# Gathering expert rows as quarter rows of a permuted copy, and turning them on VectorE instead of TensorE

## The chip, the cores and the metric
One NeuronCore of a Trainium2 chip runs the whole program. The metric is the device time of one execution in microseconds. TensorE multiplies matrices, VectorE and ScalarE do element-wise work, GpSimd issues the indirect transfers (gathers and adds by row number), SyncE issues the plain ones.

## The reference
One decoder layer over 1024 tokens of width 1024, in float32. A mixer (gated convolution, stick-breaking attention, gated linear attention, one output projection) is followed by `x1 = layer_norm(ALPHA * x + mix)`. Then a mixture of experts and a second layer norm:

```
scores = sigmoid(x1 @ router_w);  the best of 4 groups, the best 2 of its 4 experts
gate   = scores of the two, divided by their sum
for e in range(16):                       # every expert, D_EXPERT = 512
    h = silu(x1 @ w1[e]) * (x1 @ w3[e])
    y += gate[:, e] * (h @ w2[e])
out = layer_norm(ALPHA * x1 + y)
```

## The kernel before
The change touches the part behind the mixer. It has four stages.

Output projection and first layer norm: 8 tiles of 128 tokens. VectorE writes x1 (two buffers), SyncE stores each tile twice (`store_x1`): to `x1_scratch`, from which rows are gathered, and to `sum_scratch`, to which the experts' results are added.

Routing: VectorE computes for each token its two experts, the position of the token in each expert's list and the gates. An expert has 160 slots per pass (`TW`): 128 of them are the rows, 32 the spare slots (`TR`). For experts 0 to 2 (`DIRECT`) the lists are formed on the core itself: `slot_hits` compares positions with slot numbers (one-hot, `oneh`), `slot_tokens` on TensorE multiplies the one-hot by the token numbers, `slot_rows` on VectorE turns the sums into row numbers firstA and firstB. For experts 3 to 15 GpSimd scatters token numbers and gates to a table in DRAM (`scatter`, 16 indirect DMAs of 128 entries) and loads it back expert by expert (`load_table`).

Expert blocks: one block per expert, in order, each with the same list on each engine. The spare slots are computed differently from the rows: 32 slots leave three quarters of TensorE's output partitions unused, so four column groups of the weights run side by side (`spare_gu`, `spare_y`; quarter g of the output width stands on partitions 32g to 32g+31). Their x comes by quarter rows: partition 32g+s has columns 256g to 256g+255 of slot s's token (xgB, [128 x 256]). The rows come whole (xgA, [128 x 1024]). Products of the rows are made of three terms, hi by hi, hi by lo and lo by hi; the hi part of each 512 KB weight piece (12 pieces per expert) is made by ScalarE (`piece_hi`, eh), the lo part by VectorE (`piece_lo`, el), and for x there are xh and xl.

TensorE's list in a block b (`pe_block`): `spare_gu`; `rows_gu` of w1, then of w3; transpose of hB; transposes of the next expert's xgA (8, `x_transposes` rounds 0 and 1); transposes of hA (4); transposes of the next xgB (2, round 2); `spare_y`; the down products of the rows. ScalarE copies each transposed round out (`x_hi`, xh and xB) and VectorE forms xl (`x_lo`). VectorE's list: el of pieces 4 and 5, hB, el of 6 to 11, hA, hTl, xl of the next expert, el of its pieces 0 to 3, yA.

GpSimd's list in a step (`step`): load the table of expert b (one DMA of 128 entries, four of 32), copy the gates of expert b-2, compute the quarter ids, gather expert b's rows (xgA, xgB) as soon as the transposes of expert b-1 have read the buffer, then add the results of expert b-2 to `sum_scratch` (`add_rows`: yB, yA). Each instruction waits in this order. Gathers run two blocks ahead of their use; from expert 2 on one buffer serves them all.

Weights: SyncE loads piece p of the next expert when el and the raw products of piece p are done (`load_expert`).

The last block (`pe_last`, `dve_last`, `act_last`) runs beside the second layer norm, which starts when the adds of expert 14 have landed.

## Time and profile before

| | us |
|---|---|
| median of 3 runs | 970.53 (970.23 to 974.96) |
| span of the profiled execution | 966.3 |
| TensorE busy in the span | 915.8 |
| VectorE busy | 610.2 |
| ScalarE busy | 483.7 |
| GpSimd busy | 205.4 |
| mean granted TensorE clock, share of full | 0.985 |

The span runs from the first to the last instruction; the page gives no other time of that execution. The times of the runs are those of the whole device execution. Busy times of the engines overlap. The projections and the mixer take the first 425 us, the output projection until 525, routing until 550, the expert blocks until about 940.

### The profile page before, as it was taken

How to read it: one execution, taken by the hardware profiler on the slowest of the kernel's cores; microseconds unless marked ns; L12 is line 12 of the kernel's file. 1: busy time of each engine (PE TensorE's matmuls, PEld its weight loads, DVE VectorE, ACT ScalarE, POOL GpSimd, SP SyncE). 2: the span in 40 equal slices, each digit the busy share in tenths (PEclk: the TensorE clock that was granted, in tenths of full speed). 3: DMA queues.
4: the chain of work that ended last, by engine and by line, in shares of the span. 5: the costliest groups of instructions: out<-in, count | busy, mean ns of one | idle time of the engine just before them, and what ended most of it. 6: DMA issues, size and time to landing. Idle time of an engine off the chain costs nothing.

```text
span 966.3 us, 17168 instructions
## 1 busy us (share of the span) xinstructions
PE 915.8 (95%) x6403; PEld 720.1 (75%) x6403; DVE 610.2 (63%) x812; ACT 483.7 (50%) x779; POOL 205.4 (21%) x242
## 2 busy tenths in 40 slices
PE   8999999999999999979999899999999999999980
PEld 7778998996777777767887577777777777777760
DVE  4212833665665655677655897777777777777786
ACT  3312532225564654562222436666666666666674
POOL 3000000000000000040000186434334444444144
PEclk9999999999999999999999899999999999999995
DMA  9301120001100031049532289999999999999974
GB/s 262 70 22 44 45 61 27 1 2 44 44 22 23 23 77 44 1 137 361 214 113 100 91 203 314 371 338 320 317 316 319 324 318 318 321 318 315 321 257 169
DMA packets 102668, 168.81 MB, mean 175 GB/s; under 512 B 25532, under 2 KB 49212, under 8 KB 102608
## 3 DMA queue, kind: packets, MB, share of 16 engines
q1 hardware_dynamic: 88720, 143.74, 44.0%
q0 software_dynamic: 10848, 23.09, 9.8%
q10 hardware_dynamic: 3040, 1.19, 0.6%
q8 instruction: 37, 0.61, 0.3%
q14 instruction: 23, 0.19, 0.1%
HBM read 143.76 MB, written 24.54 MB: 174 GB/s over the span
## 4 chain that ended last, share of the span: by engine, by line
PE 85%; DVE 7%; ACT 3%; DMA 3%; issue 1%; POOL 0%; SPq 0%; ACTq 0%; POOLq 0%; DVEq 0%
PE bank L866 14%; PE bank L868 13%; PE bank L867 13%; PE pz L866 7%; PE pz L867 7%; PE pz L868 7%; PE pz L1216 6%; PE pz L1242 3%; PE pz L982 3%; PE bank L1060 3%; PE bank L1076 2%; PE bank L1204 1%; DVE el L1955 1%; DMA x_row<-in_x_dram 1%; PE bank L1015 1%
## 5 line engine op out<-in xcount | busy, mean ns | idle before, releaser
L1955 DVE TENSOR_TENSOR el<-er,eh 128x1024 fp32r<-128x1024 f32 x192 | 225.5, 1222 | 49.7 <-ACT eh L1556 48.8
L1556 ACT ACTIVATE eh<-er 128x1024 fp32r<-128x1024 f32 x192 | 190.2, 1052 | 8.6 <-PE pz L868 8.6
L1887 DVE TENSOR_TENSOR_SCAN Qs<-Qs,own 128x128 f32<-128x128 f32 (+7 forms) x48 | 65.0, 1355 | 69.7 <-ACT Qs L1443 69.7
L866 PE MATMUL bank<-xT_hi,w_hi 128*128 128x512 f32 (+1 forms) x264 | 105.6, 400 | 1.9 <-DVE xT_lo L1772 1.9
L868 PE MATMUL bank<-xT_hi,w_lo 128*128 128x512 f32 (+1 forms) x264 | 101.7, 385 | 0.0
L866 PE MATMUL pz<-eh,xh 128*128 128x512 f32 x256 | 101.6, 397 | 0.0
L867 PE MATMUL bank<-xT_lo,w_hi 128*128 128x512 f32 (+1 forms) x264 | 101.1, 383 | 0.0
L867 PE MATMUL pz<-el,xh 128*128 128x512 f32 x256 | 99.8, 390 | 0.0
L868 PE MATMUL pz<-eh,xl 128*128 128x512 f32 x256 | 99.7, 389 | 0.0
L629 POOL MEMSET rw<- 128x128 f32 x1 | 0.2, 205 | 413.4 <-DVE mix L1880 413.4
L866 PE MATMUL bank<-w_hi,xT_hi 128*128 128x384 f32 x192 | 65.0, 338 | 1.3 <-ACT kteN L1458 1.3
L868 PE MATMUL bank<-w_hi,xT_lo 128*128 128x384 f32 x192 | 64.2, 335 | 0.0
L867 PE MATMUL bank<-w_lo,xT_hi 128*128 128x384 f32 x192 | 64.2, 334 | 0.0
L1216 PE MATMUL pz<-er,xB 128*32 128x256 f32 x1024 | 60.5, 388 | 0.5 <-ACT xB L1603 0.5
L866 PEld LDWEIGHTS pz<-eh,xh 128*128 128x128 f32 x256 | 48.0, 188 | 16.2 <-issue 6.2
L866 PEld LDWEIGHTS bank<-xT_hi,w_hi 128*128 128x128 f32 x264 | 49.8, 189 | 11.8 <-DVE xT_lo L1772 2.1
L868 PEld LDWEIGHTS bank<-xT_hi,w_lo 128*128 128x128 f32 x264 | 49.6, 188 | 10.5
L867 PEld LDWEIGHTS bank<-xT_lo,w_hi 128*128 128x128 f32 x264 | 49.8, 189 | 8.6
L868 PEld LDWEIGHTS pz<-eh,xl 128*128 128x128 f32 x256 | 48.1, 188 | 10.2
L867 PEld LDWEIGHTS pz<-el,xh 128*128 128x128 f32 x256 | 48.1, 188 | 9.3
L866 PE MATMUL bank<-eh,hTh 128*128 128x512 f32 x128 | 51.8, 405 | 0.0
L1216 PEld LDWEIGHTS pz<-er,xB 128*32 128x32 f32 x1024 | 32.0, 111 | 26.3 <-issue 6.9
(336 smaller groups left out, 1808.5 us busy)
## 6 DMA issues: line engine op xcount, KB each, us to landing
er<-in_w_dram SPq DMA_DIRECT2D x192, 512.0 KB, 8.9
w_raw<-in_w_in_dram SPq DMA_DIRECT2D x21, 512.0 KB, 3.9
x_row<-in_x_dram SPq DMA_DIRECT2D x8, 512.0 KB, 9.0
xres<-in_x_dram SPq DMA_DIRECT2D x8, 512.0 KB, 5.4
x_scratch<-x SPq DMA_DIRECT2D x8, 512.0 KB, 2.6
sum_scratch<-x SPq DMA_DIRECT2D x8, 512.0 KB, 3.9
cx<-sum_scratch SPq DMA_DIRECT2D x8, 512.0 KB, 8.6
out_dram<-cx SPq DMA_DIRECT2D x5, 512.0 KB, 3.0
```

The lines of the kernel that those rows point to most:

```text
L866: pe.matmul(dst, lh, rh, start=(k == k_first), stop=False)
L867: pe.matmul(dst, lh, rl, start=False, stop=False)
L868: last = pe.matmul(dst, ll, rh, start=False, stop=(k == k_last))
L982: last = pe.matmul(pz[h][:, c:e], q[r, 0, own], q[r, 1, c:e], start=True, stop=True)
L1015: pe.matmul(pa_[:, h * GLA_DV:(h + 1) * GLA_DV], sT[:, h % 2, h // 2, :], gv[:, c, h * GLA_DV:(h + 1) * GLA_DV], start=(h == 0), stop=Fals ...
L1060: last = pe.matmul(po[64 * h:64 * h + 64, 0:P], sv[keys, j, (2 * p + h) * SB_D:(2 * p + h + 1) * SB_D], aT[keys, h, j, :], start=(j == 0), ...
L1076: last = pe.transpose(tr_bank[g % 2][:, (j % 4) * P:(j % 4 + 1) * P], Bs[:, n % 2, h, j * P:(j + 1) * P], ident[:, :])
L1216: last = pe.matmul(guB[g * TR:(g + 1) * TR, :].rearrange("p (m f) -> p m f", m=2), xB[:, k, :], both, start=(k == 0), stop=(k == NK - 1), ...
L1242: last = pe.matmul(yB_bank[g * TR:(g + 1) * TR, :], hTB[:, f, :], er[:, p, g * DQ:(g + 1) * DQ], start=(f == 0), stop=(f == NF - 1), skip_ ...
L1556: act.activation(eh[:, p, :], er[:, p, :], ACT.Copy).then_inc(S["eh_ok"], 1)
L1887: dve.tensor_tensor_scan(Qs[:, h, 0:W][:, ::-1], Qs[:, h, 0:W][:, ::-1], own1[:, T - W:][:, ::-1], 0.0, ALU.mult, ALU.max).then_inc(S["sca ...
L1955: dve.tensor_tensor(el[:, p, :], er[:, p, :], eh[:, p, :].bitcast(F32), ALU.subtract).then_inc(S["el_ok"], 1)
```

## The change
x1 is stored to `x1_scratch` with its columns permuted: ScalarE copies each tile (`x1_blocked`) so that quarter g of a stored row holds, for each of the 8 blocks of 128 columns, its columns 32g to 32g+31. All rows are then gathered as quarter rows: partition 32g+s of part c has quarter g of slot 32c+s. There are NB = 5 parts of [128 x 256] per expert, four for the rows and one (the last) for the spare slots, each an indirect DMA of its own. Each 32x32 block then has to be turned in place only, and VectorE's transpose does that: `spare_turn` writes xB, `rows_turn` writes xT, in one instruction each. The TensorE transposes of xgA and xgB go away, and with them ScalarE's copies from PSUM; `x_hi` is one copy of 1024 columns, `x_lo` one subtraction.

In routing, hits, token sums and row numbers are formed in two parts, the spare slots first, and token numbers are summed for each of the five parts on four partition groups (160 small matmuls per expert instead of 40). The tables have all five parts' entries on each partition. Some empty matmuls (`spin`) are added. TensorE's list in a block becomes: `spare_gu`, `rows_gu` of w1, transpose of hB, `rows_gu` of w3, half of `spare_y`, transposes of hA, the other half, hi products of the first two down pieces, then their lo products, then the rest.

```diff
-        xgAs = [rt("xgA0", 6 * K, [P, D]), rt("xgA1", 42 * K, [P, D])]
+        xg = [rt("xg0", 6 * K, [P, NB, DQ]), rt("xg1", 42 * K, [P, NB, DQ])]
+        xT = rt("xT", 16 * K, [P, NK, P])
...
+            def store_blocks(i):
+                sp.wait_ge(S["x1p_ok"], i + 1)
+                sp.dma_start(x1_dram[i * P:(i + 1) * P, :], x1p[:, i % 2, :]).then_inc(S["x1p_st"], 16)
...
             def first_gather(b):
+                pool.wait_ge(S["first_ok"], 2 * b + 1)
+                pool.indirect_dma_start(xg[b % 2][:, NB - 1, :], None, x1_quarters, bass.IndirectOffsetOnAxis(firstQ[:, b, NB - 1:NB], 0))\
+                    .then_inc(S["xgB_in"], 16)
                 pool.wait_ge(S["first_ok"], 2 * b + 2)
+                for c in range(NB - 1):
+                    pool.indirect_dma_start(xg[b % 2][:, c, :], None, x1_quarters, bass.IndirectOffsetOnAxis(firstQ[:, b, c:c + 1], 0))\
+                        .then_inc(S["xg_in"], 16)
 
             first_gather(0)
-            pool.wait_ge(S["xg_in"], 16)
+            pool.wait_ge(S["xgB_in"], 16)
+            pool.wait_ge(S["xg_in"], 16 * (NB - 1))
             first_gather(1)
             scatter(0)
             scatter(1)
...
             def load_table(r, b):
                 for g in range(NQ):
-                    pool.dma_start(tab[r][g * TR:(g + 1) * TR, 2:4], idl_dram[bass.ds(b * TW + P, TR), :]).then_inc(S["idx_in"], 16)
+                    pool.dma_start(tab[r][g * TR:(g + 1) * TR, 2:].rearrange("s (c o) -> s c o", c=NB),
+                                   idl_dram[bass.ds(b * TW, TW), :].rearrange("(c s) o -> s c o", c=NB)).then_inc(S["idx_in"], 16)
...
             def gather(r, b, buf=0, ready=None):
-                pool.indirect_dma_start(xgAs[buf][:, :], None, x1_dram, bass.IndirectOffsetOnAxis(tab[r][:, 0:1], 0)).then_inc(S["xg_in"], 16)
-                pool.indirect_dma_start(xgBs[buf][:, :], None, x1_quarters, bass.IndirectOffsetOnAxis(tabQ[r][:, 0:1], 0)).then_inc(S["xg_in"], 16)
+                pool.indirect_dma_start(xg[buf][:, NB - 1, :], None, x1_quarters, bass.IndirectOffsetOnAxis(tabQ[r][:, NB - 1:NB], 0))\
+                    .then_inc(S["xgB_in"], 16)
+                for c in range(NB - 1):
+                    pool.indirect_dma_start(xg[buf][:, c, :], None, x1_quarters, bass.IndirectOffsetOnAxis(tabQ[r][:, c:c + 1], 0))\
+                        .then_inc(S["xg_in"], 16)
...
+            def spare_turn(b, buf):
+                dve.wait_ge(S["xgB_in"], 16 * b + 16)
+                if not first_block(b):
+                    dve.wait_ge(S["raw_done"], NPIECE * (b - 1) + 2 * NF)
+                dve.transpose(xB[:, :, :].rearrange("p k s -> p (k s)"), xg[buf][:, NB - 1, :]).then_inc(S["xBt_ok"], 1)
+
+            def rows_turn(b, buf):
+                dve.wait_ge(S["xg_in"], 16 * (NB - 1) * b + 16 * (NB - 1))
+                if not first_block(b):
+                    dve.wait_ge(S["piece_done"], (NPIECE - 1) * (b - 1) + 2 * NF)
+                dve.transpose(xT[:, :, :].rearrange("p k (c s) -> p c k s", c=NB - 1),
+                              xg[buf][:, 0:NB - 1, :].rearrange("p c (k r) -> p c k r", k=NK)).then_inc(S["xTt_ok"], 1)
...
             def dve_block(b, nxt, buf=0, nbuf=0):
                 dve.tensor_tensor(hB[:, :], silB[:, :], guB[:, P:2 * P], ALU.mult).then_inc(S["hB_ok"], 1)
+                if nxt and not first_block(b):
+                    spare_turn(b + 1, nbuf)
                 piece_lo(b, 6)
                 piece_lo(b, 7)
...
                 dve.tensor_tensor(hA[:, :], silA[:, :], uA, ALU.mult).then_inc(S["hA_ok"], 1)
                 if first_block(b):
                     piece_lo(b, NPIECE - 2)
+                    spare_turn(b + 1, nbuf)
+                if nxt:
+                    rows_turn(b + 1, nbuf)
                 dve.wait_ge(S["hTh_ok"], b + 1)
```

## Rows read from the trace of the kernel before

**Rows 1.** The page: busy us, share of the span, instructions.

```profile
PE 915.8 (95%) x6403; PEld 720.1 (75%) x6403; DVE 610.2 (63%) x812; ACT 483.7 (50%) x779; POOL 205.4 (21%) x242
```

**Rows 2.** Chain of waits, spare products of experts 1 and 14: start, us, what.

```profile
580.81 3.59 PE pz L1216 x64
...
891.38 3.59 PE pz L1216 x64
```

**Rows 3.** Timeline of TensorE, end of a block: start us, us, group.

```profile
786.57 1.03 PE L1204 MATMUL bank<-ident,xgA 128*128 128x128 f32 x8
787.44 0.61 PE L1301 MATMUL pz<-ident,hA 128*128 128x128 f32 x4
787.89 0.38 PE L1204 MATMUL pz<-ident,xgB 128*128 128x128 f32 x2
788.20 1.93 PE L1242 MATMUL pz<-er,hTB 128*32 128x256 f32 x32
...
795.75 3.66 PE L1216 MATMUL pz<-er,xB 128*32 128x256 f32 x64
```

**Rows 4.** Stretches: length, busy (x) of PE, PEld, DVE, ACT, POOL; clock, DMA, GB/s.

```profile
549.00:556.00 7.00, 6.04 (x82) 3.28 (x80) 5.58 (x23) 0.60 (x2) 2.72 (x3) 0.54 0.48 128
...
604.70:628.60 23.90, 23.90 (x188) 17.97 (x191) 17.45 (x19) 15.53 (x21) 10.45 (x12) 1.00 1.05 370
...
867.50:891.40 23.90, 23.90 (x187) 17.97 (x191) 17.52 (x19) 15.61 (x21) 10.33 (x11) 1.00 0.95 315
```

**Rows 5.** Timeline of VectorE in the same blocks; in brackets the idle time before.

```profile
786.65 0.69 DVE L2219 TENSOR_TENSOR hA<-silA,pz 128x512 f32<-128x512 f32 x1 [1.51 <-PE pz L868]
...
799.80 0.28 DVE L2205 TENSOR_TENSOR hB<-silB,pz 128x128 f32<-128x128 f32 x1
800.74 4.63 DVE L1955 TENSOR_TENSOR el<-er,eh 128x1024 fp32r<-128x1024 f32 x4 [0.65 <-ACT eh L1556]
```

**Rows 6.** Timeline of GpSimd, gathers of experts 2 and 3 and between.

```profile
582.56 2.04 POOL L689 DMA_INDIRECT xgB<-x_scratch,firstB  x1 [0.30 <-issue]
...
590.12 1.20 POOL L723 DMA_DIRECT2D tab<-slot_tokens  x1
590.72 2.64 POOL L725 DMA_DIRECT2D tab<-slot_tokens  x4
600.09 0.68 POOL L731 TENSOR_SCALAR tabQ<-tab,quad 128x1 uint32<-128x1 uint32 x1 [6.73 <-DMA tab<-slot_tokens]
601.63 1.18 POOL L739 DMA_INDIRECT xgA<-x_scratch,tab  x1 [0.86 <-POOL tabQ L731]
...
605.31 1.63 POOL L707 DMA_INDIRECT sum_scratch<-yB,addB  x1 [0.30 <-issue]
...
608.53 1.21 POOL L723 DMA_DIRECT2D tab<-slot_tokens  x1
...
617.77 0.30 POOL L731 TENSOR_SCALAR tabQ<-tab,quad 128x1 uint32<-128x1 uint32 x1 [6.00 <-DMA tab<-slot_tokens]
```

**Rows 7.** Scatters (ns min/median/max, first and last start), and timelines beside el.

```profile
L678 POOL DMA_INDIRECT slot_tokens<-tokg,rows_u x16: 968/1097/2034, 556.2 to 581.3; - x16
...
576.68 2.03 POOL L678 DMA_INDIRECT slot_tokens<-tokg,rows_u  x1 [0.30 <-issue]
579.02 1.97 POOL L678 DMA_INDIRECT slot_tokens<-tokg,rows_u  x1 [0.31 <-issue]
...
576.65 4.62 DVE L1955 TENSOR_TENSOR el<-er,eh 128x1024 fp32r<-128x1024 f32 x4
```

**Rows 8.** Timelines of GpSimd, VectorE and TensorE at the first block.

```profile
552.91 1.03 POOL L689 DMA_INDIRECT xgB<-x_scratch,firstB  x1 [3.89 <-DMA xgA<-x_scratch,firstA]
...
556.41 1.29 DVE L1961 TENSOR_TENSOR xl<-bank,xh 128x512 fp32r<-128x512 f32 x2 [1.31 <-ACT xh L1603]
...
557.98 0.50 PE L866 MATMUL pz<-eh,xh 128*128 128x512 f32 x1
```

**Rows 9.** DMA issues: KB, median us from issue to landing.

```profile
xgB<-sum_scratch,tabQ POOLq DMA_INDIRECT x1, 6.6
```

More of the change, by code:

```diff
@@ L258, in build @@
         oneb = small("oneb", [P, P], BF16)
-        tab = [small(f"tab{r}", [P, 4], U32) for r in range(4)]
-        tabQ = [small(f"tabQ{r}", [P, 1], U32) for r in range(4)]
+        tab = [small(f"tab{r}", [P, 2 + 2 * NB], U32) for r in range(4)]
+        tabQ = [small(f"tabQ{r}", [P, NB], U32) for r in range(4)]
         slotGs = [small(f"slotG{r}", [P, 2]) for r in range(2)]
@@ L277, in build @@
         addB = small("addB", [P, DIRECT], U32)
[L278 to L281 removed]
+        assert place[0] <= R + 53 * K, place[0] - R - 53 * K
         selm = at("selm", C0 + 5760, [P, P])
@@ L318, in build @@
         oneh = rt("oneh", 24 * K, [P, 2, NT, TW], BF16)
+        place[0] = M + 29 * K
+        sids = small("sids", [P, DIRECT, NB])
+        firstQ = small("firstQ", [P, DIRECT, NB], U32)
+        sidA = small("sidA", [P, DIRECT])
+        assert place[0] <= M + 30 * K
         er = at("er", R, [P, NPIECE, D])
@@ L1189, in _, with spare_gu @@
             slot_gates(0)
+            spin(4, po[:, 0:GLA_W])
             slot_tokens(1)
             slot_gates(1)
-            def x_transposes(b, rounds, buf=0):
-                xgA, xgB = xgAs[buf], xgBs[buf]
-                if first_block(b) and rounds == (2,):
-                    pe.wait_ge(S["xgB_in"], 16)
-                else:
-                    pe.wait_ge(S["xg_in"], 32 * b + 16)
-                for r in rounds:
-                    for d in range(4 if r < 2 else 2):
-                        rows = xgA[:, (4 * r + d) * P:(4 * r + d + 1) * P] if r < 2 else xgB[:, d * P:(d + 1) * P]
-                        last = pe.transpose(xb[r][:, d * P:(d + 1) * P], rows, ident[:, :])
-                    last.then_inc(S["xtr_ps"], 1)
-            def spare_gu(b, part=None):
-                for q in range(NF) if part is None else range(2 * part, 2 * part + 2):
+            spin(4, po[:, 0:GLA_W])
+            def spare_gu(b):
+                pe.wait_ge(S["xBt_ok"], b + 1)
+                for q in range(NF):
                     for p in (q, NF + q):
@@ L1302, in pe_block, with products @@
                 last.then_inc(S["hTA_ps"], 1)
-                if nxt:
-                    x_transposes(b + 1, (2,), nbuf)
-                spare_y(b)
-                pe.wait_ge(S["hTl_ok"], b + 1)
-                if not first_block(b):
+                spare_y(b, range(2, NF))
+                if first_block(b):
+                    pe.wait_ge(S["first_ok"], 6)
+                else:
                     pe.wait_ge(S["yA0_ev"], b)
                     pe.wait_ge(S["yA1_ev"], b)
-                for f in range(NF):
+                pe.wait_ge(S["hTh_ok"], b + 1)
+                def products(f, half, low):
                     p = 2 * NF + f
-                    pe.wait_ge(S["el_ok"], NPIECE * b + p + 1)
-                    for half in range(2):
-                        last = mm3(pe, pp[half][:, :], 0, NF - 1, lambda f: (hTh[:, f, :], hTl[:, f, :]),
-                                   lambda f: (k_of(eh, p, half), k_of(el, p, half)), [f])
+                    if low:
+                        last = pe.matmul(pp[half][:, :], hTl[:, f, :], k_of(eh, p, half), start=False, stop=(f == NF - 1))
                         if f == NF - 1:
@@ L1320, in pe_block @@
                             last.then_inc(S["piece_done"], 1)
+                    else:
+                        pe.matmul(pp[half][:, :], hTh[:, f, :], k_of(eh, p, half), start=(f == 0), stop=False)
+                        pe.matmul(pp[half][:, :], hTh[:, f, :], k_of(el, p, half), start=False, stop=False)
+                for f in range(2):
+                    pe.wait_ge(S["el_ok"], NPIECE * b + 2 * NF + f + 1)
+                    for half in range(2):
+                        products(f, half, False)
+                pe.wait_ge(S["hTl_ok"], b + 1)
+                for f in range(2):
+                    for half in range(2):
+                        products(f, half, True)
+                for f in range(2, NF):
+                    pe.wait_ge(S["el_ok"], NPIECE * b + 2 * NF + f + 1)
+                    for half in range(2):
+                        products(f, half, False)
+                        products(f, half, True)
             def pe_pass(j):
-                if isinstance(j, int):
-                    pe.wait_ge(S["first_ok"], 4)
-                    x_transposes(0, (2,))
-                else:
+                if not isinstance(j, int):
                     pe.wait_ge(S["hA_ok"], NE * j)
-                    x_transposes(NE * j, ROUNDS_FIRST)
                 experts_of(pe, j, pe_block, pe_last)
```

255 lines of the change are left out of this document (128 added, 127 removed).

## The prediction
> **What bounds the kernel now.** I read the page's busy shares first: TensorE is busy for 95% of the span [rows 1]. Then the loop over the 16 experts, because the change touches that and the short stage ahead of it. The chain of waits runs through TensorE: its 64 spare-slot products start at 580.81 us for expert 1 and at 891.38 for expert 14 [rows 2], so a block takes (891.38 - 580.81) / 13 = 23.89 us. The timeline of TensorE across the end of a block shows no gap [rows 3]. The other engines and the transfers have room: VectorE is busy 17.5 us of a block, and the load is 315 GB/s where the same loop reached 370 in an earlier block [rows 4]. So the loop is as long as TensorE's instruction list, as long as what feeds it comes in time. What feeds it is a long line of steps on GpSimd (table load, gather, adds of an earlier expert), hidden today.
>
> **Part 1, what TensorE loses.** Eight transposes of xgA run from 786.57 to 787.44, two of xgB from 787.89 to 788.20 [rows 3]: 0.87 + 0.31 = 1.18 us per block. A block that only TensorE limits takes 23.89 - 1.18 = 22.71 us. The removed work also covered waits, so I go through the new order. After the last gate/up product VectorE needs about 1.0 us for hA (the transposes of hA start at 787.44, hA at 786.65 [rows 3, 5]); two quarters of spare_y (half of its 1.87 to 1.93 us, 0.93 [rows 3]) now stand there, a loss of at most 0.1. The other half stands behind the transposes of hA, while ScalarE copies hTh. Eight hi products (8 x 0.23 = 1.8 us) stand before hTl is wanted. VectorE puts the new turn of the rows between hA and hTl: the turn may take about 2.5 us before TensorE notices. x1's permuted copy costs ScalarE one more 1024-column copy per tile in a stage in which it is idle most of the time: nothing, and its store replaces one that was there.
>
> **Part 2, what VectorE gains.** No 32x32 turn is in the trace. The nearest rows are 1024-column operations in SBUF, el at (4.63 / 4) 1.16 us [rows 5]; upper end: twice that, 2.3 us, if the type takes two passes; lower end half of it, 0.6 us, if two columns go at once. I take 1.2 for the rows and, with a quarter of the columns, 0.4 for the spare slots. xl becomes one operation instead of two, the same time. VectorE then works 17.5 + 1.6 = 19.1 of 22.7 us: it fits. The Trainium skill ("Vector Engine (DVE) Microarchitecture Reference", 3.8 The reshape front-end) says that the transpose sustains one element per cycle per lane; that agrees with my middle value, and no run here shows it yet. ScalarE's three copies per block become one over 1024 columns: a small gain, hidden, since ScalarE is busy for 15.6 of 23.9 us [rows 4].
>
> What can hurt is the place of spare_turn in VectorE's queue. It stands behind hB, before el of pieces 6 to 11, and waits for the spare gather of the next expert. hB starts at 799.80, 4.05 us into a block (block start 795.75 [rows 3, 5]). Six el at 1.16 us stand behind it, 7.0 us, and hA is wanted at 14.8 us into the new block (3.6 spare products, 0.1 hB transpose, 11.0 gate/up, 0.1). So spare_turn has to be through by 7.8 us; from there every us is lost by TensorE.
>
> **Part 3, GpSimd, which I hold to be the point that decides.** One step of it, in order: gather (2 issues before, 5 now), add of yB, add of yA, table load, wait for the table, quarter ids. In the one step that waited for nobody else, gathers start at 601.63, the adds at 605.31, the table load at 608.53, the ids at 617.77 [rows 6]: 3.68 for two gathers, 3.22 for the adds (I take 3.3, for the copy of the gates that later steps have beside them), 9.24 for the table (9.97 in the step before it, 590.12 to 600.09; I take the middle, 9.6), and 1.54 from the ids to the next gather (600.09 to 601.63) [rows 6]. Without gathers: 3.3 + 9.6 + 1.5 = 14.4 us. The tables now carry 5 entries per row instead of 1 in four small DMAs; the issue of 128 entries takes 1.20 us and the four of 32 entries take 2.64 together [rows 6], so the 160 entries that each now has cost between nothing and 0.5 us apiece. I take 0.15, nearer to the row in which four times the entries hardly show: 0.6 for the four. Sum 15.0.
>
> What is a gather issue worth? Sixteen scatters of the same form start within 25.1 us, 1.67 apart on the mean, durations 0.97 to 2.03 [rows 7]. The long ones stand where VectorE runs el back to back: 576.68 and 579.02 start inside the run of four el from 576.65 and end 2.3 us apart; where VectorE reads PSUM or is idle the spacing is 1.3 [rows 7]. The Trainium skill ("SBUF — State Buffer", Who interferes with whom) has the rule that a VectorE instruction with two SBUF inputs contends with a GpSimd instruction that reads SBUF; the trace agrees (2.03 against 0.97 us). By it the four new gathers per block cost up to 2.3 each. Bounds for five gathers: 5 x 1.3 = 6.5 and 1.3 + 4 x 2.3 = 10.5. I take 7.8 us: a gather that is late is issued while VectorE itself stands waiting at spare_turn, with only two el in the way. Step: 15.0 + 7.8 = 22.8 us, against 22.71 of TensorE: level, bounds 21.5 and 25.5.
>
> **Part 4, the start.** Before, hi/lo row products start at 557.98, behind xl at 556.41 [rows 8]. After: the spare hits (256 columns compared first instead of 1280 at once) let the first spare gather go about 1.2 us earlier, but the four row gathers follow at 1.3 to 1.5 each behind the rest of the count and land at about 555.5 (before: xgA had landed at 552.9, when GpSimd went on [rows 8]). Then the turn 1.2, the rest of the routing chain and one el that stand between (3.1) and xl (1.2): row products at 561.0, 3.0 us later. Block 0 also gets 120 more small matmuls (about 1 us) and loses the 1.5 us of transposes: it ends at 584 instead of 580.8. TensorE's clock was at half for most of 549 to 556 (0.54 on the mean [rows 4]); the added spins may spare that, the new wait may bring it back: plus or minus 3, taken as none.
>
> GpSimd starts its 16 scatters late: first_gather(1) waits until the first gathers landed (555.5) and issues five (7.5 us): 563 instead of 556.2, so expert 2's gather starts at 589.8 instead of 582.56 [rows 6], and expert 3's at 589.8 + 19.07 (601.63 - 582.56) + 4.4 + 0.6 = 613.9. A gather under load lands 6.6 us after its issue [rows 9], with the mean delay to its wait about 7. So in block 1 spare_turn(2) waits until 596.8, 12.8 us into the block: 5.4 lost. In block 2, spare_turn(3) waits until 620.9; six el, hA, its transposes, spare_y and the down products (5.7, from 790.1 to 795.75 [rows 3]) follow (0.3 + 7.0 + 0.8 + 0.45 + 0.93 + 5.7 = 15.2, less 0.3 of overlap): block 2 ends at 635.8. Twelve blocks at 22.8 follow: block 14 ends at 909.4. Before it ended at 891.38 + 23.89 = 915.3. That is 5.9 us less. The last block and the layer norm behind it have none of the removed work except what block 14 held: unchanged. The span of the profiled execution is 966.3 us; the median of the runs, 970.53, stands 4.2 above it; I take the difference from the median: 970.5 - 5.9 = 964.6 us.
>
> **Rivals.** (A) TensorE's list alone decides: gathers stay at 1.3 apart and the start catches up. Block 0 ends at 584, fourteen blocks at 22.71 end at 901.9: -13.4, 957 us. For it: the low spacing stands in half of the rows. Against: the five gathers in a row at the start. Chance 0.15.
> (B) Slower: GpSimd's line becomes the bound. The new gathers fall on el, 2.3 apart; five take 9.1, the step is 15.0 + 9.1 = 24.1 us or more; block 14 ends at 635.8 + 12 x 24.1 = 925: +9.7, 980 us. The turning point is a step of (915.3 - 635.8) / 12 = 23.3 us, only 0.5 above my sum. Sign of it: VectorE waits in every block at spare_turn, TensorE has gaps ahead of the transposes of hA. By the skill's port rule without the relief that I assumed, this is the outcome. Chance 0.20.
> (C) The turn of [128 x 1024] costs two passes or more (over 2.5 us): hTl is late in each block and the start loses 1 to 3 more: 970 to 985. Chance 0.07.
> (D) Steps level near 23.2: the removed 1.2 us per block are given back to waits, 967 to 972. Chance 0.18.
> My forecast, 0.40, its own range 960 to 968.
>
> **How the numbers follow.** A comparison of such runs tells about 0.5% (4.85 us) from no change. Below 965.7: all of A, two thirds of the forecast and a little more, 0.15 + 0.30; some of the rest lies where the start is cheaper than I made it: 0.47. Above 975.4: B, most of C: 0.27. Between: 0.26. Range: 955 to 981, which leaves a tenth on either side.
>
> **What would show it.** Blocks at 22.7 to 23.0 us instead of 23.89; five gather issues in 6.5 to 8; the ids of the next table 9 to 11 us behind the table load; a stop of VectorE ahead of the [128 x 256] turn in blocks 1 and 2, about 8 us in block 1, and a short one in the later ones; expert 2's first gather near 590. The turn of 1024 columns at 1.1 to 1.3 us. I am wrong if there is no such stop (then A), or if blocks are over 23.3 us (then B).

## The result: 0.7% slower, and the profile after

| us | before | after |
|---|---|---|
| median, 5 runs each on one chip | 970.23 (967.71 to 974.96) | 977.50 (972.44 to 981.02) |
| span of the profiled execution | 966.3 | 979.3 |
| TensorE busy | 915.8 | 913.9 |
| GpSimd busy | 205.4 | 284.0 |
| mean granted clock | 0.985 | 0.973 |

The ratio is 1.0070 [1.0047, 1.0093]: 0.7% slower, with the whole interval above 1. I had forecast 964.6. The profiled execution of the changed kernel is the slowest of its five runs (981.02), so the two spans stand 13.0 us apart and the medians 7.3. The account of the 13.0 us below is one of these two executions.

The page's busy rows of the changed kernel, against [rows 1]; GpSimd has 50 more instructions, TensorE is busy as long as before:

```profile
PE 913.9 (93%) x6611; PEld 707.4 (72%) x6611; DVE 631.5 (64%) x831; ACT 482.2 (49%) x755; POOL 284.0 (29%) x292
```

One block of TensorE, its timeline from one spare_gu to the next, against [rows 3] (the products of the rows are left out). The ten transposes are gone, and in a block that waits for nothing 23.09 us are left of 23.89:

```profile
756.33 3.66 PE L1226 MATMUL pz<-er,xB 128*32 128x256 f32 x64
...
765.50 0.28 PE L1294 MATMUL pz<-ident,hB 128*128 128x128 f32 x1
...
771.16 1.07 PE L1253 MATMUL pz<-er,hTB 128*32 128x256 f32 x16
772.16 0.66 PE L1300 MATMUL pz<-ident,hA 128*128 128x128 f32 x4
772.75 1.07 PE L1253 MATMUL pz<-er,hTB 128*32 128x256 f32 x16
...
779.42 1.93 PE L1226 MATMUL pz<-er,xB 128*32 128x256 f32 x32
```

But many blocks wait. VectorE's waits over blocks 1 to 14 (what, in all us, times, longest): it stands before the turn of the next expert's spare rows, 8.0 us once and 28.2 us in eleven blocks. TensorE pays for the long stops alone: block 1 takes 28.9 us and four later blocks take 24.4, 23.4, 25.4 and 27.0; all others take 23.1.

```profile
DVE xB L1982 <- DMA xg<-x_scratch,tabQ: 28.2, 11, 5.4
...
DVE xB L1982 <- DMA xg<-x_scratch,firstQ: 8.0, 1, 8.0
```

VectorE's timeline has the stop of block 1 and both turns, 0.45 and 1.24 us, against the el beside them [rows 5]:

```profile
601.06 0.45 DVE L1982 STREAM_TRANSPOSE xB<-xg 128x256 f32<-128x256 f32 x1 [8.04 <-DMA xg<-x_scratch,firstQ]
...
771.88 1.24 DVE L1989 STREAM_TRANSPOSE xT<-xg 128x1024 f32<-128x1024 f32 x1
```

GpSimd's timeline of one step, against [rows 6]. The step's first gather started at 734.84; from there 6.8 us of gathers, 4.3 of adds, 9.9 from the table load to the ids, 2.7 from the ids to the next gather. From the first gather of expert 3 to that of expert 15 it waits for nobody but its own table:

```profile
741.62 2.64 POOL L774 DMA_INDIRECT sum_scratch<-yB,tabQ  x1 [0.30 <-issue]
744.56 1.89 POOL L779 DMA_INDIRECT sum_scratch<-yA,tab  x1 [0.30 <-issue]
745.91 1.18 POOL L737 DMA_DIRECT2D tab<-slot_tokens  x1
...
755.77 1.75 POOL L746 TENSOR_SCALAR tabQ<-tab,quad 128x5 uint32<-128x5 uint32 x1 [6.12 <-DMA tab<-slot_tokens]
758.51 1.09 POOL L756 DMA_INDIRECT xg<-x_scratch,tabQ  x1 [0.99 <-POOL tabQ L746]
```

Expert 3's first gather starts at 613.38 and expert 15's at 902.10: 288.72 / 12 = 24.06 us a step, over the 23.89 of the whole block before. Means over these steps: gathers 7.2 us, adds 4.1, table 9.8, ids to gather 2.9.

Where 13.0 us of span went, by the starts of spare_gu in TensorE's timeline (the last column from the prediction's 584, 22.71 + 5.4, and 909.4):

| stretch | before | after | difference | predicted |
|---|---|---|---|---|
| start of block 1 | 580.8 | 587.4 | +6.6 | +3.2 |
| block 1 | 23.9 | 28.9 | +5.0 | +4.2 |
| blocks 2 to 14 | 310.6 | 308.0 | -2.6 | -13.3 |
| block 15 to the last GpSimd issue | 46.1 | 45.7 | -0.4 | 0 |
| last issue to the end of the span | 5.0 | 9.4 | +4.4 | 0 |

### The profile page after: what moved, and what is told of

Same layout as the page of the kernel before. It is cut to its first block, busy times and chain, and to the rows that moved or that the text cites. A ratio compares the mean times of both kernels' runs of the same rounds, so it can differ in the third digit from the quotient of the medians.

```text
span 979.3 us, 17611 instructions
## 1 busy us (share of the span) xinstructions
PE 913.9 (93%) x6611; PEld 707.4 (72%) x6611; DVE 631.5 (64%) x831; ACT 482.2 (49%) x755; POOL 284.0 (29%) x292
## 4 chain that ended last, share of the span: by engine, by line
PE 56%; POOL 16%; DMA 10%; issue 8%; DVE 6%; ACT 3%; POOLq 0%; SPq 0%; DVEq 0%; ACTq 0%
PE bank L887 11%; PE bank L889 11%; PE bank L888 11%; DMA tab<-slot_tokens 9%; PE pz L1003 3%; PE bank L1081 2%; POOL xg L759 2%; POOL tabQ L746 2%; PE pz L887 2%; PE pz L889 2%; PE pz L888 2%; PE bank L1097 2%; POOL sum_scratch L774 2%; POOL sum_scratch L779 2%; POOL slot_tokens L685 2%
## 5 line engine op out<-in xcount | busy, mean ns | idle before, releaser
L887 PE MATMUL pz<-eh,xh 128*128 128x512 f32 x256 | 104.4, 408 | 4.4 <-DVE el L1975 4.4
L759 POOL DMA_INDIRECT xg<-x_scratch,tabQ x52 | 58.3, 1122 | 15.9 <-issue 15.9
L889 PEld LDWEIGHTS bank<-xT_hi,w_lo 128*128 128x128 f32 x264 | 49.9, 189 | 10.6
L889 PEld LDWEIGHTS pz<-eh,xl 128*128 128x128 f32 x256 | 48.6, 190 | 10.6
```

The costliest lines, as they stand in the source:

```text
L759: pool.indirect_dma_start(xg[buf][:, c, :], None, x1_quarters, bass.IndirectOffsetOnAxis(tabQ[r][:, c:c + 1], 0))\
L887: pe.matmul(dst, lh, rh, start=(k == k_first), stop=False)
L889: last = pe.matmul(dst, ll, rh, start=False, stop=(k == k_last))
```

## The experiments

There were 18 runs. Those of one group shared a chip, each group had another one, and each run is compared with the kernel before on its chip. The changed kernel itself ran in the first comparison and in the second group only. "Changed" is the kernel after the change.

### First group: the step of GpSimd, and the place of the turn

**One row gather.** Three of the four row gathers are left out from expert 3 on, so three quarters of xT hold old rows.

```diff
-                for c in range(NB - 1):
+                for c in range(1):
```


> The changed kernel, but from expert 3 on GpSimd issues one row gather instead of four per expert (three quarters of the rows keep what an earlier expert left there; everything else, tables included, is unchanged). Theory 1 (GpSimd's step bounds the loop): its step falls from 24.06 us by three issues of about 1.35, to 20.0; TensorE's own list, 23.1 us per block, decides again and the stops of VectorE at the turn of the spare rows end after block 2: 12 blocks at 23.1 instead of 24.06, some 8 us less than the changed kernel, 969 to 970 us. Theory 2 (only the start costs, the loop is fine): no change, 977. Theory 3 (the loop is slow because the 1 KB rows crowd the DMA queues): also about 8 us less, since 0.38 MB per block goes away with the issues; the next kernel tells 1 from 3.

Measured: 984.84 against 974.07, ratio 1.0104 [1.0069, 1.0139]. It is slower, not 8 us faster, and yet from block 1 on every block takes 23.1 us and no stop at the spare turn is left, as the step theory says. (The theory of crowded transfers says so too; the table a step ahead, below, keeps all transfers and tells them apart.) The loss is in block 0, which took 47.1 us. TensorE's timeline there, in the middle of 200 small products (slot_tokens and slot_gates of expert 2), shows a few at a time:

```profile
577.56 0.22 PE L1191 MATMUL bank<-idb,oneh 128*32 128x2 bf16 x6 [0.51 <-issue]
578.30 0.21 PE L1191 MATMUL bank<-idb,oneh 128*32 128x2 bf16 x4 [0.52 <-issue]
579.01 0.22 PE L1191 MATMUL bank<-idb,oneh 128*32 128x2 bf16 x5 [0.50 <-issue]
...
588.36 0.23 PE L1204 MATMUL bank<-gsplit,oneh 128*32 128x4 bf16 x4 [1.19 <-issue]
```

**Table a step ahead.** The table of expert b+1 is loaded behind the gathers of b, ahead of the adds.

```diff
+                    load_table(0, 4)
...
+                    for b in range(4, NE):
+                        quarters(b % 4, b)
+                        gather(b % 4, b)
+                        if b + 1 < NE:
+                            load_table((b + 1) % 4, b + 1)
+                        if b > 4:
+                            gates((b + 2) % 4, b - 2)
+                            add_rows((b + 2) % 4, b - 2)
...
-                with pool.Fori(2 if isinstance(j, int) else 1, NE // 4) as i:
```

The edit also writes out GpSimd's steps of experts 8 to 15, which had been a loop. That is not what shortens the step: in the changed kernel the steps written out (first gather of expert 3 to that of expert 8, 613.38 to 734.84) take 24.3 us each and those in the loop (734.84 to 902.10) 23.9.

> The changed kernel with GpSimd's list reordered: the table of the next expert is loaded right behind the gathers and ahead of the two adds, so that its landing (9 to 10 us from the issue) passes beside the adds. Same transfers, same bytes, same number of issues. Theory 1: the step becomes ids 2.9 + gathers 7.1 + table issue 3.6 + adds 4.3 + a rest of the landing of about 2 = 20 us, below TensorE's 23.1; about 8 us less than the changed kernel, 969 to 970. Theory 2 (start only) and theory 3 (queues crowded by small rows): no change, 977.

Measured: 1028.62, ratio 1.0557. Block 0 took 46.5 us; blocks 1 to 3 took 23.1 to 23.3, the later ones 27.2 (the last 24.3). That was my edit: gates(b-2) now stood behind the gather of b, which waits for the rows' turn, and ScalarE's yB waits for those gates. Its waits:

```profile
ACT yB L1653 <- POOL slotG L764: 81.3, 10, 8.1
```

**Spare turn late.** spare_turn moves from behind hB to behind hA.

```diff
-                if nxt and not first_block(b):
-                    spare_turn(b + 1, nbuf)
...
                 if nxt:
+                    spare_turn(b + 1, nbuf)
                     rows_turn(b + 1, nbuf)
```


> The changed kernel with the turn of the spare rows moved in VectorE's list from ahead of the six el to behind hA, next to the turn of the rows. GpSimd's step stays at 24 us. Theory 1: the stop of 8 us in block 1 no longer reaches TensorE (5.8 us gained there), but the steps of 24 us catch up in the later blocks, where now the turn of the rows waits: the end moves by the difference of the two deadlines only, about 4 us less than the changed kernel, 973 to 974, and the blocks from 8 or so on take 24 us. Theory 2 (start only): 5.8 us less and all later blocks at 23.1: 962 to 965.

Measured: 1008.89, ratio 1.0323; block 0 46.0, then blocks of 23.1 to 26.7. The later deadline moved the wait: ScalarE's yB now waited 37.3 us in ten blocks for the landing of yA's adds. How much of the time over the forecast is that and how much is block 0 can't be told, since the changed kernel did not run on this chip.

**Kernel before with five gather issues.** Three more quarter-row gathers per expert from expert 3 on, into places that nobody reads.

```diff
+                for q in range(3):
+                    pool.indirect_dma_start(junk[q][:, :], None, x1_quarters, ...tabQ[r][:, 0:1]...)
```


> The kernel before with three more indirect gathers of quarter rows per expert from expert 3 on, into a buffer that nobody reads: five issues as in the changed kernel, 0.38 MB more per block. Theory 1: GpSimd's step grows from about 18 to 22 to 23 us and stays below the 23.89 of TensorE's block: no change, 970 to 971. Theory 3 (transfers crowded): slower by 3 us or more.

Measured: 979.85 against 974.07, ratio 1.0081 [1.0046, 1.0117]. I had expected no change; the 3 us or more that the crowded-transfer theory asked for came. But blocks take 24.0 us instead of 23.9 and two early ones 24.3 and 24.9, some 2.4 us over blocks 1 to 14. So three more gathers are nearly hidden, with GpSimd's step now level with the block (24.0). Block 0 took 33.4 us and the end of the span 7.0 instead of 5.0; what block 0 of the kernel before takes on this chip was not profiled.

### Second group: is it the variant or the run, and where do the pauses come from

**Changed kernel again.**


> The changed kernel as it is, once more. Block 0 took 29.0 us in its first profile, but 46.0 to 47.1 in the three variants that differ from it only on GpSimd or in the place of a turn, with TensorE's program the same. If what differs between those runs is the run (where the program's instructions lie, the chip), this one shows it: block 0 over 40 us and a time near 990. If the variants caused it: block 0 about 29 us and a ratio near 1.007 as before.

Measured: 1000.93 against 983.99, ratio 1.0188 [1.0133, 1.0242], and block 0 took 47.2 us. So the variants were not the cause; what the chip or the run brings with it is. Four blocks took 26.0 to 26.9 us for want of rows. Its TensorE had pauses among ordinary products too (row of line 1226), and longest in the small ones:

```profile
569.46 2.81 PE L1226 MATMUL pz<-er,xB 128*32 128x256 f32 x12 [0.37 <-issue]
...
583.95 0.21 PE L1191 MATMUL bank<-idb,oneh 128*32 128x2 bf16 x2 [1.93 <-issue]
584.66 0.16 PE L1191 MATMUL bank<-idb,oneh 128*32 128x2 bf16 x1 [0.51 <-issue]
```

**Third expert's counts early.** slot_tokens(2) and slot_gates(2), and VectorE's hits for them, move ahead of block 0.

```diff
             slot_gates(1)
+            slot_tokens(2)
+            slot_gates(2)
```


> The 200 small products of the third expert's counts and gates moved from the middle of block 0 to before it, on VectorE too. Theory 4 (TensorE runs out of instructions in a long row of small products while the weights load): block 0 takes about 24 to 26 us without pauses in TensorE's list and starts 2 us later, so the kernel gains 2 us against the changed kernel where that had 29 us, and some 20 where that had 47. Rival (block 0 waits for the weights anyway): block 1 starts where it did.

Measured: 1007.97, ratio 1.0246 [1.0184, 1.0308], 7 us over the changed kernel. Block 0 itself took 28.0 us, but began at 584.8: the row of small products had the same pauses in its new place. From 570 to 585 the DMA engines moved next to nothing there (share 0.02, scatters alone) and TensorE was busy for 3.45 of 15 us, so the loads of weights around the row are not what does it.

**Table a step ahead, gates first.** The diff is against the first variant with the table ahead.

```diff
+                        if b > 4:
+                            gates((b + 2) % 4, b - 2)
                         quarters(b % 4, b)
                         gather(b % 4, b)
...
                         if b > 4:
-                            gates((b + 2) % 4, b - 2)
                             add_rows((b + 2) % 4, b - 2)
```


> As the variant with the table a step ahead, but each step copies the factors of the expert two before first, so that ScalarE's spare row doesn't wait for a gather. If the step of GpSimd (24.06 us) bounds the loop and the table's wait of 9.8 us is its largest part, the step shrinks to about 15 us, blocks 2 to 14 take 23.1 us each, there is no stop at the spare turn, and the time is 8 us under the changed kernel's with the same block 0. If landing of the rows or of the additions bounds it: blocks stay at 23.7 or more.

Measured: 987.91, ratio 1.0047 [1.0017, 1.0077]: still over the kernel before, and 13.0 us under the changed kernel beside it. All blocks from 1 on take 23.1 us but one of 23.3. I expected 8; the changed kernel's loop had lost more than that on this chip (block 15 started at 944.1, here at 930.5).

**Kernel before with more small products.** Expert 2's count of spare rows in block 0 is repeated four times more.

```diff
-                for i in range(NT):
+                for i in [i for _ in range(5 if b == 2 else 1) for i in range(NT)]:
```


> The kernel before, with the third expert's count of spare rows repeated four times more in block 0: 128 further small products, 208 in a row instead of 80. Theory 4: TensorE's list has pauses of 0.5 to 1.2 us among them and block 0 takes 5 to 20 us more; the kernel is 5 to 20 us slower than before. Rival (a small product costs only its 0.01 us here, and the pauses belong to the changed kernel's other edits): 1 to 2 us slower, no pauses.

Measured: 986.70, ratio 1.0044 [1.0011, 1.0076]; block 0 took 47.1 us, 16 pauses of 10.9 us in all stood in the row, and all other blocks took 23.9. The same pauses, then, without anything of the change. The pauses also cost clock: the granted clock was 0.50 from 575 to 583 and still 0.60 from 583 to 590, when TensorE was busy throughout:

```profile
575.00:583.00 8.00, 2.42 (x104) 1.91 (x103) 0.53 (x5) 0.00 (x0) 3.90 (x4) 0.50 0.86 151
583.00:590.00 7.00, 7.00 (x20) 5.50 (x21) 3.88 (x21) 0.00 (x0) 2.47 (x2) 0.60 0.34 101
```

That it raised the median by only 2.7 us suggests that most runs of the kernel before have the pauses on this chip already (18 of its 23 runs lie between 981.8 and 987.5, five between 974.4 and 979.0); it was not profiled here.

### Third group: counting with fewer products

**Kernel before again.**


> The kernel before as it is, for its profile on this chip. If long rows of small products lose more on some chips than on others, its block 0 (80 small products) takes between the 29.5 us of its first profile and the 47 us of the variant with 208, and TensorE's list shows pauses of 0.5 to 1.2 us in lines 1167 to 1184; all its other blocks take 23.9 us.

Measured: 969.29, ratio 0.9994 [0.9985, 1.0003]. On this chip block 0 takes 29.5 us and no pause shows.

**Few counts.** The hits are summed once (8 products for the rows, 8 for the spare slots), and one product with `selm`, which has a one wherever two row numbers are equal modulo 32, spreads the sums over the quarters: 35 small products per expert instead of 200.

```diff
-                            for g in range(NQ):
-                                last = pe.matmul(sids_bank[b % 2][1 - part][g * TR:(g + 1) * TR, 2 * c:2 * c + 2],
+                        last = pe.matmul(bank[:, 4:4 + NQ], selm[:, :], tidq[:, b, :], start=True, stop=True, ...)
```


> The changed kernel with the counts in two stages: the hits of the 128 rows are summed once in 8 products, and one product with a matrix of ones in the places of equal row number spreads the numbers over the four quarters, so that an expert takes 35 small products instead of 200. Theory 4 (TensorE runs out of instructions in a long row of small products): block 0 takes about 24 to 26 us without pauses over 0.6 us, and the kernel gains 3 us on a chip on which the changed kernel's block 0 takes 29 us, and about 20 where it takes 47. Rival (weights or the scatters hold block 0): it takes as long as in the changed kernel.

Measured: 976.88, ratio 1.0079 [1.0051, 1.0108]. There was nothing to win here: the pauses are absent on this chip. The rest of the loss (block 1 at 32.1 us, the step, the end) stands. Counting in two stages has a price of its own: VectorE's stop at the spare turn in block 1 is 11.1 us, where the kernel with the long row (table ahead again, below) has 8.1.

**Few counts and table ahead.**


> The counts in two stages and the next expert's table loaded behind the gathers. If the two losses of the changed kernel are the step of GpSimd and the pauses of TensorE and nothing else: block 1 starts by 585, all blocks from then on take 23.1 us, and the kernel ends at 955 to 962 us, about 1% under the kernel before. Rival (one of them only moves the wait): over 965.

Measured: 973.93, ratio 1.0040 [1.0025, 1.0054], not under 962. Blocks 2 to 14 take 23.1 us, but block 1 took 32.9. The table ahead gave 3.0 us against few counts alone, and that was not enough to come under the kernel before.

**Table ahead again.**


> The table a step ahead alone, once more, on the chip of the other three: its difference to the one with both is what the counts in two stages give, 3 us where block 0 takes 29 us and about 20 where it takes 46.

Measured: 972.83, ratio 1.0035 [1.0022, 1.0049], 1.1 us under the one with few counts; I had expected it 3 over. So few counts gain nothing on a chip without the pauses. The chain of waits of this kernel and of the one before on this chip (spare_gu of block 2, and of block 14 or 15) shows 23.09 us a block, and block 15 three us earlier than before, at 914.25 instead of 917.4:

```profile
614.13 3.59 PE pz L1228 x64
...
914.25 3.59 PE pz L1228 x64
```

```profile
606.95 3.59 PE pz L1216 x64
...
893.61 3.59 PE pz L1216 x64
```

GpSimd's timeline in it: the ids are ready early, and the gather waits for the turn that frees its buffer, no longer for the table.

```profile
742.06 0.88 POOL L746 TENSOR_SCALAR tabQ<-tab,quad 128x5 uint32<-128x5 uint32 x1 [0.37 <-DMA tab<-slot_tokens]
747.20 1.07 POOL L756 DMA_INDIRECT xg<-x_scratch,tabQ  x1 [4.25 <-DVE xT L1991]
```

Yet the spans are 969.1 and 969.3 (the fastest run of this kernel and the slowest of the other; the medians are 3.5 apart the other way). The three us come back behind the last GpSimd issue, which stands 9.2 us ahead of the end here and 5.0 there:

```profile
959.93 0.97 POOL L849 DMA_INDIRECT out_dram<-cx,rest_u  x1 [0.30 <-issue]
```

```profile
964.35 0.97 POOL L826 DMA_INDIRECT out_dram<-cx,rest_u  x1 [0.30 <-issue]
```

### Fourth group: the end, and expert 2's gather

**Kernel before with a longer skipped pass.** GpSimd's program has a branch for further passes, which these inputs never need; 24 semaphore instructions per gather are added inside it.


> From the last GpSimd issue to the end of the span the kernel before takes 5.0 us, the changed kernel and its variants 9.0 to 9.4, the one with one row gather 6.1, the kernel before with three more gathers 7.1. Between them differs only GpSimd's program. Here the kernel before gets 192 further semaphore instructions in the pass that GpSimd skips at the end (it is for more tokens than these inputs have, and never runs). Theory 5 (the jump over a longer body costs more at the end): the end takes 7 to 10 us and the kernel 2 to 5 us more. Rival (the end depends on what was written or awaited last): 5.0 us as before, ratio 1.000.

Measured: ratio 1.0057 [1.0009, 1.0105], but that is the mix of two groups of runs (five from 973.2 to 973.8, seven from 985.3 to 986.9), and its end takes 6.2 us: 1.2 more, less than I said. The profiled execution, 985.32, is one of the upper group: its block 0 takes 44.2 us, with 10.3 us of pauses.

**Table ahead, expert 2's gathers between the scatters.**

```diff
             scatter(0)
-            scatter(1)
             ...
             first_gather(2)
+            scatter(1)
```


> The table a step ahead, and expert 2's gathers put between the two scatters instead of behind both. If block 1's loss of 5.8 us comes from the 16 scatters ahead of that gather: block 1 takes 23.1 us where it took 28.9, block 2 at most 1 more, and the time is 5 to 6 us under the variant with the table ahead alone (ratio about 0.998 on a chip on which block 0 takes 29 us). Rival: expert 3's gather is now late and block 2 loses the 5.8.

Measured: 986.31, ratio 1.0078 [1.0033, 1.0123]. The profile has a block 0 of 47.2 us, which covers the gather anyway; it can't tell. The runs fall into two groups, five from 976.2 to 979.1 and seven from 985.9 to 988.6.

**The same with few counts.**


> The same with the counts in two stages (35 small products for an expert instead of 200). Theory 4: on a chip on which block 0 takes 46 us without it, it takes about 30 here, 15 us less; on one on which it takes 29, nothing or 1 us less. Block 0 after that is as long as VectorE and the weights make it.

Measured: 973.94, ratio 0.9979 [0.9941, 1.0017]. Against the variant with the long row on the same chip, 12.4 us less in the median, of which that one's upper group makes the most: its lower group is some 5 us over this one. Block 0 takes 32.6 us instead of 47.2. Block 1 still takes 30.4: VectorE is no longer stopped at the spare turn but 10.6 us at hB (below).

**And a shorter skipped pass.** Three row gathers are left out of the pass that never runs.


> The same with GpSimd's skipped pass shortened: three of the four row gathers left out of it (it never runs with these inputs). Theory 5: the end takes 6 us instead of 9.3 and the kernel is 3 us faster. Rival: no change.

Measured: 973.83, ratio 0.9988 [0.9955, 1.0020], and its end takes 8.6 us where the other had 8.5. Theory 5 falls as the reason for the longer end.

### Fifth group

**Kernel before with few counts** for expert 2.

```diff
-                    for g in range(NQ):
+                    for g in range(NQ if b < 2 else 1):
...
+                pe.matmul(pp[1][:, 4:5], selm[0:TR, :], sids[0:TR, 8:9], start=True, stop=True, ...)
```


> The kernel before with the counts of expert 2, which stand inside block 0, in two stages: 34 small products there instead of 80. Theory 4: on a chip on which runs of the kernel before fall into two groups 11 us apart, all runs of this one lie in the lower group; where before has only one group, it is equal (ratio 0.998 to 1.002). Rival (the groups have another cause): two groups here too.

Measured: 977.07 against 984.40, ratio 0.9963 [0.9925, 1.0001]. Two groups remain (973.6 to 978.4, eight runs; 981.2 to 982.9, four), the upper one less often and lower. Its profile has block 0 at 36.2 us with pauses left among ordinary products. The one-group forecast did not come true, its direction did: with fewer small products, fewer runs lie in the upper group.

**Few counts, table ahead, split, again.**


> The changed kernel with counts in two stages, the table a step ahead and expert 2's gathers between the scatters, once more. From the run before: one group of runs, 974 us, level with the lower group of the kernel before (ratio 0.998 to 1.003 to it), 10 us under the upper group where there is one.

Measured: 974.48 (969.13 to 976.95) against 984.40 (974.33 to 987.66), ratio 0.9908 [0.9877, 0.9939]. On this chip the mended change is 0.9% under the kernel before. Three quarters of that are the counts: the kernel before with few counts for expert 2 alone, at 977.07, leaves 2.6 us. The changed kernel was not run here.

## Why the prediction was wrong, point by point

**Part 1, TensorE's list.** I said 22.71 us; it is 23.09. All ten transposes went, but blocks that wait for nothing gained 0.80 us, not 1.18. What the list got in place of them is visible only in part (some 0.2 us): spare_y now runs in two halves with the transposes of hA between, 1.0 + 0.6 + 1.0 us from 771.16 to 773.75, where 32 products in one row had taken 1.93 with the transposes 0.45 [rows 3]. The term was too large by 0.38, 4.9 us over 13 blocks; where the rest of it goes is open.

**Part 2, VectorE.** Right. The turns take 1.24 and 0.45 us against 1.2 and 0.4, so a turn is as dear as an el of the same width (1.22), which agrees with the Trainium skill ("Vector Engine (DVE) Microarchitecture Reference", 3.8 The reshape front-end). hTl was on time in every block. The stop at spare_turn came where I put it: 13.7 us into block 1 (I said 12.8), and block 1 took 5.8 us over its 23.1 (5.4).

**Part 3, GpSimd's step: the step that failed.** 22.8 us predicted, 24.06 measured, and my own turning point was 23.3. By the means, gathers were cheaper (7.2 against 7.8) and the table a little (9.8 against 10.2). What was wrong are the two terms that I carried over from a step of before: the adds, 4.1 instead of 3.3, and the way from the ids to the gather, 2.9 instead of 1.5. The ids went from one column to five. With five columns they took 0.27 us where VectorE was idle (802.46, variant with gates first), but 1.3 to 2.35 in the changed kernel, where from expert 4 on they stand beside el in every step; the one column of [rows 6] had taken 0.68 beside el and 0.30 behind it. The add of yB took 1.63 us in [rows 6], mostly ahead of el; in the changed kernel it takes 2.3 to 2.65 where el runs all along beside it (2.64 in the step shown) and 1.63 where el runs for part of it. That the adds and ids are longer because of el was not tested by itself.

Blocks 2 to 14 came out 10.7 us over the forecast: 4.9 are part 1 and 5.8 the stops that a longer step brings. That it is the step is shown from two sides: one row gather instead of four, or the table a step ahead, each give blocks of 23.1 us without a stop, and the table ahead was worth 13.0 us on one chip and 3.0 on another. But it is not the whole loss. Between the forecast (5.9 us under before) and the profiled executions (13.0 over) lie 18.9 us: 5.8 of the step, 4.9 of TensorE's list, 4.4 of the end, 3.4 of the start, 0.8 of block 1, less 0.4. Without the step's 5.8 the sum would still have come out slower, as the table ahead did on every chip on which it ran by itself (ratios 1.0047 and 1.0035).

**Part 4, the start.** The row products start at 563.38, not 561.0, and block 1 at 587.35, not 584. The clock, "taken as none", is a part of it. The windows of after (columns as in [rows 4]) have it at 0.50 and 0.56 until 562, where before had 0.54 [rows 4] and 1.00 from 556 to 562:

```profile
549.00:556.00 7.00, 5.54 (x221) 3.55 (x219) 5.18 (x18) 0.00 (x0) 4.84 (x4) 0.50 0.27 80
556.00:562.00 6.00, 5.32 (x76) 2.47 (x80) 5.66 (x14) 2.34 (x2) 3.73 (x3) 0.56 0.25 69
```

The 120 more small products, "about 1 us", are the other thing that was mis-sized. On the chip of the first comparison 2.4 us of pauses stand among them, one of 2.09 us ahead of block 0; on others block 0 takes 46 to 47 us. Their share in the 3.4 us and that of the clock were not told apart.

**The end, "unchanged".** From block 15 to the last issue that held (45.7 against 46.1). Behind it 4.4 us were lost, which no step of mine looked at. All 13 profiles of kernels with the change and all its gathers have 8.5 to 9.4 us there, the kernel before and its two variants with other counts 5.0. The traces show what stands there: a closing instruction of GpSimd named DRAIN, which ends at 979.06 after and at 966.02 before; the last instructions of all engines follow it by 0.1 to 0.3 us. Of line L141 (ns min/median/max, start), after and before:

```profile
L141 POOLq DRAIN  x1: 6740/6740/6740, 972.3 to 972.3; - x1
...
L141 POOLq DRAIN  x1: 1290/1290/1290, 964.7 to 964.7; - x1
```

Its length goes with the number of indirect DMAs that GpSimd has issued in the program: 1.2 to 1.3 us after 85 (kernel before and its variants without more gathers), 3.7 after 94 (one row gather), 4.5 after 124 (before with five issues), 6.2 to 6.8 after 133 (all kernels with the change). The skipped pass had no part in it (1.2 us with the longer one, whose 1.2 us more lie ahead of the DRAIN; 6.2 with the shorter). Why it takes longer stays open; no run varied the number of DMAs alone.

**The rivals.** B (0.20) forecast a step of 24.1 us, a stop at spare_turn in the later blocks and 980 us. The step and the stops came, the time in part (977.5), and the agreement is luck. B's sum doesn't follow from its own premise: gathers 2.3 us apart make 10.5 for five, by my bounds, not 9.1, and a step of 25.5. In the step shown they stand 1.25 to 1.6 apart. Nor are the 7.3 us of the medians B's 9.7 in the loop: 4.4 of the spans' difference is the end. A is what the table a step ahead makes of the loop, though at 23.09.

## The mended version beside the kernel before

Few counts, table ahead and split lie at 974 us on two chips, within 969 to 979, where the kernel before lay between 970 and 988 (one outlying run of each left aside). On one of the two that is no difference (0.9979 [0.9941, 1.0017]), on the other 0.9% less. To the lower group of the runs of before (970.1 to 975.8 in the fourth group) they are level, so the gain is that of the counts, and a kernel before with few counts for all three experts, which was not run, may do as well. What the turn gives in the loop, 13 x 0.80 = 10.4 us, goes back: the profile of the fifth group against that of before in the third (another chip) has 2.0 us more at the start of block 0, 3.4 in it, 6.7 in block 1 and 3.5 at the end.

## What to carry to other kernels

Where a change lengthens a line of steps that is hidden, sum the whole line from one stretch in which the engines beside it do what they will do then; here two terms read in a quiet stretch were 0.8 and 1.4 us short, and that put the line over the bound. Then look at the stages outside the loop with the same care: the start and the end together missed the forecast by 7.8 us here, the line by 5.8. If the sum is level with the bound, look first for a wait in the line that can be started a step earlier (here the table's 9.9 us) before counting issues. And count instructions, not only their time: the block with the row of 200 small products took 29.0 us on one chip and 47.2 on another.

## What the runs showed of the hardware

**TensorE can pause in a long row of small products, waiting for nothing that the profile shows.** For some 20 us around block 0 (562 to 590) it gets groups of 1 to 7 small products every 0.72 or 1.4 us; rows of full products in the same spell mostly lose 0.3 to 0.8 now and then (one stop of 5.8 in the variant with expert 2's gathers between the scatters). The pauses sum to 0 us in both profiles of the kernel before, 2.4 in the changed kernel of the first comparison, 10 to 25 in nine other profiles and 0 to 5 in the rest. On the chip of the fourth group the kernel before itself has two groups of runs: 21 of 35 from 970.1 to 975.8 and 13 from 982.8 to 988.4 (one at 5187 us apart). Of its changed forms, the one with the long row has two groups as well; the two with few counts stay at 970 to 976 but for two of 24 runs (979.0 and 1168). So the small products bring the pauses out. Why they come on some chips and in some runs only is not shown.

I first read them as TensorE running out of instructions. The Trainium skill ("Runtime: NRT & Kernel Launch", Instruction fetch mechanics) says that the fetch of instructions is hidden by the issue floor. The traces don't show the contrary: they record instruction transfers as queues of their own (q8 and q14), and none runs where the pauses are densest. In the variant with the third expert's counts early, 15 pauses make 11.8 of the 15 us from 570 to 585. The stretch, and all queues that its DMA view lists:

```profile
570.00:585.00 15.00, 3.45 (x58) 2.26 (x60) 0.49 (x1) 0.00 (x0) 11.35 (x13) 0.50 0.02 1
...
q0 software_dynamic: 383, 0.01, 2.1%
```

These are GpSimd's scatters. The variant with one row gather has 11 pauses from 582 to 593 and no instruction transfer from 582 to 606. So the pauses there are no wait for a recorded transfer of instructions, and no full transfer path either; what they are stays open.

**A spell of full DMA engines at low bandwidth.** With few counts and expert 2's gathers between the scatters, block 1 loses its us all the same (30.4 us). The windows of that kernel (fourth group) show the 16 engines full at 66 GB/s, where the one with the table ahead alone moved 256 in the same five us at a share of 0.89. VectorE's hB waits for ScalarE's silB, which starts at 603.16 after a wait of 11.7 us. By the kernel silB waits for the spare products alone, but the timeline has them ended by 593.7 and the view names no releaser, so what held it is not shown. Scatters of 8 bytes an entry are issued until 599; whether they are what fills the engines wasn't tried.

```profile
595.00:600.00 5.00, 4.53 (x18) 2.88 (x16) 0.00 (x0) 0.00 (x0) 3.78 (x5) 1.00 1.01 66
600.00:605.00 5.00, 1.99 (x9) 1.31 (x9) 1.22 (x3) 1.84 (x3) 2.47 (x2) 1.00 1.05 164
```
